# Two column units of the second block as matmuls over halves of the rows

## What is computed

```python
h = rmsnorm(x, g_mix[l])
proj = h @ w_in[l]
xc, gb, gc, q, k, v, g_sw, gate_a, gate_r = jnp.split(proj, split_points, axis=-1)
...
qf = rotary(q.reshape(b, s, RET_HEADS, RET_QK_DIM).astype(jnp.float32)) * (RET_QK_DIM ** -0.5)
kf = rotary(k.reshape(b, s, RET_HEADS, RET_QK_DIM).astype(jnp.float32))
vf = v.reshape(b, s, RET_HEADS, RET_V_DIM).astype(jnp.float32)
...
y_r = (ret.astype(dt) * jax.nn.silu(g_sw)) @ w_r_out[l]
```

## Time and profile before

| | |
|---|---|
| median of 3 runs | 900.77 us (899.85 to 902.6) |
| the profiled execution's own time | 902.56 us |
| its span | 900.4 us |
| TensorE busy | 888.9 us, 99% of the span, 5434 matmuls |
| TensorE weight loads | 761.2 us, 85% |
| VectorE, ScalarE, GpSimd busy | 608.1, 456.2, 82.9 us |
| DMA | 160.45 MB, mean 178 GB/s |

### The profile page before, as it was taken

One profiled execution on the slowest core, in us unless ns is written; L12 is line 12 of the kernel. 1 busy time (PEld: TensorE's weight loads), 2 busy tenths in 40 slices (PEclk: granted clock), 3 DMA queues, 4 the chain that ended last, 5 costly groups with the idle time before them and its releaser, 6 DMA issues.

```text
span 900.4 us, 12763 instructions
## 1 busy us (share of the span) xinstructions
PE 888.9 (99%) x5434; PEld 761.2 (85%) x5434; DVE 608.1 (68%) x734; ACT 456.2 (51%) x549; POOL 82.9 (9%) x93
## 2 busy tenths in 40 slices
PE   8999999999999999999999999999999999999997
PEld 8989788788888887888888888888888888888885
DVE  5989886776666567778858665766566566664665
ACT  6674553664445446555444365443355555444543
POOL 1001230100000000000124210110100000000000
PEclk9999999999999999999999999999999999999999
DMA  9764315146555543654564544355544456455531
GB/s 321 263 218 167 106 55 197 59 167 249 195 196 196 189 187 141 222 187 147 207 219 175 187 156 171 141 187 187 187 187 144 154 193 231 176 179 209 187 140 47
DMA packets 26089, 160.45 MB, mean 178 GB/s; under 512 B 3577, under 2 KB 4233, under 8 KB 8241
## 3 DMA queue, kind: packets, MB, share of 16 engines
q1 hardware_dynamic: 23616, 153.40, 46.8%
q0 software_dynamic: 2272, 6.24, 2.1%
q10 hardware_dynamic: 144, 0.00, 0.0%
HBM read 158.57 MB, written 2.63 MB: 179 GB/s over the span
## 4 chain that ended last, share of the span: by engine, by line
PE 83%; DVE 9%; ACT 3%; issue 2%; DMA 1%; SPq 1%; POOL 0%; POOLq 0%; DVEq 0%; ACTq 0%
PE banks L505 34%; PE banks L473 21%; PE banks L476 10%; DVE t_wl L1645 4%; PE banks L428 3%; PE banks L577 3%; PE banks L533 2%; PE banks L416 1%; PE banks L447 1%; DMA t_x<-in_x 1%; PE banks L778 1%; ACT t_wh L1155 1%; PE banks L983 1%; PE banks L1117 1%; DVE t_cv L1674 1%
## 5 line engine op out<-in xcount | busy, mean ns | idle before, releaser
L1645 DVE TENSOR_TENSOR t_wl<-t_raw,t_wh 128x2048 fp32r<-128x2048 f32 x136 | 311.7, 2313 | 109.0 <-ACT t_wh L1155 107.9
L473 PE MATMUL banks<-t_hx,t_wh 128*128 128x512 f32 x992 | 312.1, 396 | 0.0
L1155 ACT CAST t_wh<-t_raw 128x2048 fp32r<-128x2048 f32 x136 | 256.0, 1908 | 12.6 <-DMA t_raw<-in_W 7.9
L476 PEld LDWEIGHTS banks<-t_hx,t_wl 128*128 128x128 f32 x992 | 186.3, 188 | 43.7
L476 PE MATMUL banks<-t_hx,t_wl 128*128 128x256 f32 x992 | 194.9, 278 | 0.0
L473 PEld LDWEIGHTS banks<-t_hx,t_wh 128*128 128x128 f32 x992 | 153.3, 189 | 2.4
L505 PE MATMUL banks<-t_wh,t_hx 128*128 128x512 f32 x320 | 101.6, 394 | 0.0
L505 PEld LDWEIGHTS banks<-t_wh,t_hx 128*128 128x128 f32 x320 | 59.5, 188 | 12.5 <-issue 0.3
L505 PE MATMUL banks<-t_wl,t_hx 128*128 128x512 f32 x160 | 61.1, 390 | 0.0
L2293 POOL TENSOR_TENSOR t_st<-t_st,t_half 128x1 f32<-128x1 f32 (+1 forms) x18 | 10.6, 590 | 434.2 <-DVE t_st L1674 425.7
L1483 ACT COPY t_hold<-banks 128x512 f32<-128x512 f32 x28 | 16.4, 585 | 65.2 <-PE banks L476 54.6
(11 more groups left out here) (334 smaller groups left out, 1330.6 us busy)
## 6 DMA issues: line engine op xcount, KB each, us to landing
t_raw<-in_W SPq DMA_DIRECT2D x139, 1024.0 KB, 4.8
t_raw<-in_W SPq DMA_DIRECT2D x8, 256.0 KB, 6.3
t_raw<-in_W SPq DMA_DIRECT2D x4, 512.0 KB, 9.5
skew<-scr POOLq DMA_DIRECT2D x1, 1536.0 KB, 13.5
t_cout<-in_xT SPq DMA_DIRECT2D x4, 256.0 KB, 5.1
t_x<-in_x SPq DMA_DIRECT2D x2, 512.0 KB, 11.1
t_tab<-in_tab POOLq DMA_DIRECT2D x1, 640.0 KB, 7.6
out<-t_xt SPq DMA_DIRECT2D x2, 320.0 KB, 2.3
```

What stands on the lines that cost most here:

```text
L473: e.matmul(bank[b + c], M.wh[:, h, wk], M.hx[:, k, :, :].rearrange("p a s -> p (a s)"), start=k == 0, stop=False)
L476: m = e.matmul(bank[b + c][:, 0:S], M.wl[:, h, wk], M.hh[:, k, :], start=False, stop=k == 7)
L1155: e.copy(M.wh[:, h, :], M.raw[:, r, :]).then_inc(q.sem, q.tick(("hi", i)))
L1645: e.tensor_tensor(M.wl[:, h, :], M.raw[:, r, :], M.wh[:, h, :].bitcast(F32), ALU.subtract).then_inc(q.sem, q.tick(("lo", i)))
```

## The change

A function `wide_rows` takes two B units at once and multiplies them in four phases. In each phase two banks are filled for half of the rows each: the upper 64 rows of all 8 blocks go to bank f of the four, the lower 64 rows to bank f + 2 (modulo 4). So four phases give each bank both of its halves, each matmul has 64 rows in place of 128, and there are 128 of them in place of 64. At the start of phase f TensorE waits for the end of its own phase f - 2. Before phase 0 it waits for lo and for the banks of both units, and it signals both units at the end of phase 3. It replaces `wide_unit` for rot(h, 0) with rot(h, 1), and for g(h, 0) with g(h, 1): 8 pairs. A further function `a_rows`, not called anywhere, is left out of the diff below. ScalarE's, VectorE's, GpSimd's and SyncE's programs are not edited.

```diff
+            def wide_rows(tiles, arrived, by, names, places=(None, None)):
+                banks, slots = [], []
+                for tile, to in zip(tiles, places):
+                    if to is None:
+                        turn[0] += turn[0] % 2
+                    b, i = take(tile, to), next_unit()
+                    if to is None:
+                        take((tile, 1))
+                    assert PLAN[i][0] == "B" and b % 2 == 0, (i, PLAN[i], tile)
+                    q.wait_ge(DV, ("lo", i))
+                    opened(b)
+                    opened(b + 1)
+                    banks += [b, b + 1]
+                    slots.append(i)
+                for f in range(4):
+                    enter(2)
+                    for k in range(8):
+                        arrived(k)
+                        for w in range(2):
+                            for half in range(2):
+                                g = (f + 2 * half) % 4
+                                p, h, b = slice(64 * half, 64 * half + 64), slots[g // 2] % HR, banks[g]
+                                wk = slice(k * 256 + g % 2 * 128, k * 256 + g % 2 * 128 + 128)
+                                if w == 0:
+                                    e.matmul(bank[b], M.wh[p, h, wk], M.hx[p, k, :, :].rearrange("p a s -> p (a s)"),
+                                             start=f < 2 and k == 0, stop=False)
+                                else:
+                                    m = e.matmul(bank[b][:, 0:S], M.wl[p, h, wk], M.hh[p, k, :], start=False,
+                                                 stop=f >= 2 and k == 7)
+                    if f < 3:
+                        next_phase(m)
+                m.then_inc(q.sem, q.tick(*tiles, *[("unit", i) for i in slots], ("phase", phase[0])))
+                phase[0] += 1
+                for n, (b, name) in enumerate(zip(banks[::2], names)):
+                    drain(b, by, name)
+                    drain(b + 1, by, name)
...
-            def rotate(h, w):
-                wide_unit(("rot", h, w), x_mix2, DV, ("turned0", h, w))
+            def rotate(h):
+                wide_rows((("rot", h, 0), ("rot", h, 1)), x_mix2, DV, (("turned0", h, 0), ("turned0", h, 1)))
...
             for h in range(4):
-                rotate(h, 0)
-                rotate(h, 1)
+                rotate(h)
...
-            wide_unit(("g", 0, 0), x_mix2, DV, ("gsm", 0, 0))
-            wide_unit(("g", 0, 1), x_mix2, DV, ("gsm", 0, 1))
+            wide_rows((("g", 0, 0), ("g", 0, 1)), x_mix2, DV, (("gsm", 0, 0), ("gsm", 0, 1)))
...
-                for u in range(2):
-                    if h:
-                        wide_unit(("g", h, u), x_mix2, DV, ("gsm", h, u))
+                if h:
+                    wide_rows((("g", h, 0), ("g", h, 1)), x_mix2, DV, (("gsm", h, 0), ("gsm", h, 1)))
```

More of the change, by code:

```diff
@@ L388, in tensor @@
             q.begin(e)
-            free, turn, unit = [None] * 8, [0], [0]
+            free, turn, unit, phase = [None] * 8, [0], [0], [0]
             def take(tile, b=None):
@@ L483, in wide_unit, with next_phase, enter, a_rows @@
                 drain(b + 1, by, name)
+            def next_phase(last):
+                last.then_inc(q.sem, q.tick(("phase", phase[0])))
+                phase[0] += 1
+            def enter(back):
+                if phase[0] >= back:
+                    q.wait_ge(PE, ("phase", phase[0] - back))
+            def a_rows(name, act, arrived, ks, outs, first):
+                i = next_unit()
+                assert PLAN[i][0] == "A", (i, PLAN[i], name)
+                h = i % HR
+                q.wait_ge(DV, ("lo", i))
+                for k in ks:
+                    arrived(k)
+                banks = [outs[t][c] for t in range(2) for c in range(2)]
+                if first:
+                    for b in banks:
+                        opened(b)
+                for f in range(4):
+                    enter(2)
+                    for kk, k in enumerate(ks):
+                        for a, w in ((0, 0), (0, 1), (1, 0)):
+                            for half in range(2):
+                                g = (f + 2 * half) % 4
+                                p, t, c = slice(64 * half, 64 * half + 64), g // 2, g % 2
+                                m = e.matmul(bank[banks[g]][:], act[a][p, k, t * 128:t * 128 + 128],
+                                             W[w][p, h, kk * 1024 + c * 512:kk * 1024 + c * 512 + 512],
+                                             start=first and f < 2 and kk + a + w == 0, stop=False)
+                    if f < 3:
+                        next_phase(m)
+                m.then_inc(q.sem, q.tick((name, 0), (name, 1), ("unit", i), ("phase", phase[0])))
+                phase[0] += 1
```

## The result

The changed kernel takes 936.12 us (median of 4 runs, 933.45 to 938.16), the kernel before 900.58 us: a ratio of 1.0389 with a 95% interval of 1.0358 to 1.0420. The forecast was 930.0 us, with a range of 919.4 to 937.0.

The account below looks back on a forecast made before the run. TensorE was taken to bound the kernel. Waits 2.6 + 12.3 + 5.0 + 5.0, ways in and out 0.8 and clock 3.5 made 29.2 us; on the median 900.8 that gave 930.0 us, range 919.4 to 937.

Parts of the forecast that it names:

- The bound: TensorE, busy 99% of the span: whatever its stream gains or loses comes out in the time one for one.
- The pace of a couple: In the pairs, two matmuls of 64 rows side by side take as long as one of 128: no gain, no loss.
- rival 1: The waits come, and couples of 64-row matmuls run faster: 5.8 to 7.1 us less, 923.5; chance 0.32.
- rival 2: The waits come, and couples run slower, each half paying its 0.014 us: 937; chance 0.09.
- rival 3: The halves don't run side by side, so 8 pairs take 22 in place of 11 us: 1019; chance 0.05.
- One sign: In the pairs, the two matmuls of a couple start a few ns apart, couples 0.23 and 0.12 us apart.
- The joint waits: TensorE's waits around pairs, restarts included: 2.6 us at rot(0), 12.3 at three later pairs, 5.0 before and 5.0 behind g(1) to g(3).
- Rival 4: Not slower: second cast, lo and banks are ready within the 1.7 us of `scores`, no stops: 895; chance 0.04.
- In and out of 64 rows: At the pairs, 0.1 us in and 0.2 out where no wait covers it: 0.8 us behind four pairs.
- The clock: TensorE's clock slows behind the three stops of 4.0 us, 1.2 us lost for each: 3.5 us.
- The bounds of the clock: Slow-clock loss between nothing and 1.7 us for all seven long and short stops, 12 us.
- The 0.014 us per matmul over its columns: In TensorE's wide units, time beyond the columns at 2.4 GHz, about 0.014 us per matmul; its cause was left open.

Follow-up runs that it names:

- one unit at a time: The change with matmuls of 64 rows kept, but each unit on its own two banks, waiting for and freeing only its own: 909.17 us, ratio 1.0096.
- with A units: The kernel before, with the six wr units of heads 1 to 3 multiplied by halves of the rows, without joint waits: 901.53 us, ratio 1.0006.
- filled stops: The change plus 17 unread matmuls of 512 columns behind each of scores(0), scores(1) and scores(2), no wait removed: 929.38 us, ratio 1.0320.
- another order: The change with ScalarE and VectorE reordered at the rot pairs: both casts and lo before the taking-out, both takings-out before the rotations: 917.81 us, ratio 1.0194.
- neighbouring banks: The change with the two halves of the rows one bank apart in place of two, nothing else: 934.61 us, ratio 1.0379.
- with all rows: The change with every wait of the pairs kept, but multiplying with all 128 rows as before: 933.01 us, ratio 1.0361.

## Why the prediction was right, and where it was off

The mechanism was the one forecast, and the forecast was too low in two terms. Growth of each stretch of TensorE's timeline, from those transposes (357.69 and 355.74) on:

| stretch | before, us | after, us | growth | the sum had |
|---|---|---|---|---|
| to the first A unit behind rot(0) | 85.45 | 89.56 | 4.1 | 2.6 |
| to `scores(0)` | 33.04 | 33.52 | 0.5 | 0.2 |
| `scores(0)` to `scores(3)` | 38.62 | 58.53 | 19.9 | 16.4 |
| to the transposes at the end of head 0 | 26.26 | 26.36 | 0.1 | 0 |
| the rounds of heads 1 to 3 | 109.59 | 120.63 | 11.0 | 10.0 |
| to the end | 249.74 | 249.70 | 0 | 0 |
| all | 542.70 | 578.30 | 35.6 | 29.2 |

- **The bound.** TensorE's losses came out in the time one for one: behind the last pair the two kernels take the same time, and nothing gave a loss back.
- **The pace of a couple** was taken as that of a full matmul. At full clock two steps of 768 columns take 578.39 - 577.69 = 0.70 us in the changed kernel, as in the earlier trace rows:

```profile
577.69 0.43 PE L549 MATMUL banks<-t_hx,t_wh 64*128 64x512 f32 x2
...
578.39 0.44 PE L549 MATMUL banks<-t_hx,t_wh 64*128 64x512 f32 x2
```

  So rivals 1, 2 and 3 are out. One sign did not come as written: the two halves of a couple start a few ns apart only at first, and inside a pair they drift half a step apart, at an unchanged pace (one half at 444.15, the other at 444.36, the first again at 444.50).

  The Trainium skill's rule (TensorE: Matmul & The Clock Gate, "What overlaps and what doesn't"), by which halves would have hidden weight loads and won 7 us, fails here: the loads of full rows had been beside the matmuls all along, and the halves won nothing.
- **The joint waits** came as worked out: 2.8 once, 3.8 three times, 1.4 to 1.6 six times. The step to the next pair was 5.81 us for 5.7. Keeping the waits and dropping the halves left the loss; reordering ScalarE and VectorE took 18 us away. Rival 4, a stop covered by `scores`, is out by the same rows.
- **In and out of 64 rows** was put too low. rot(1) took 11.5 us with its way out, where 11.1 and 0.2 make 11.3, and the way in cost another 0.1 in front of it: 0.4 to 0.5 together for 0.3, as in the runs with one unit at a time and with A units (0.4). And the waits do not cover it, as the sum had it for the pairs of g(1), g(2) and g(3): each of these rounds grew by 3.7 us, of which 3.0 are waits. With the restarts these small terms make 2.0 us more than the sum had.
- **The clock is the term that was mis-sized.** "Part of each slow stretch falls into the stop itself, so I take 1.2 for each: 3.5." Measured: 2.4, 2.8 and 1.4 us behind the three long stops, and 1.3 behind the stop of 2.8 us, which the sum had left out: 7.9. Two of the stretches were much longer than the one in the earlier trace rows (5.5 and 6.3 us of the pair at 0.50). So the sum was 4.4 us too low in the clock and 2.0 in the ways in and out and the restarts, 29.2 + 6.4 = 35.6. That the clock caused its part behind the three long stops is shown by the run with the filled stops, 6.7 us faster.
- **The bounds of the clock** were wrong by their own numbers. There were ten stops in the list (one, three and twice three), not seven; and 12 us in place of 3.5 would have made 938.5, above the 937 at which the range ended. The measured 936.12 lies 0.9 us below that end.
- **What the clock was read from.** The prediction took the earlier trace rows to mean that thin work lowers the clock. The same stretch of the changed kernel was nearly as thin (23 matmuls from 20 to 24 us in place of 20), and the clock stayed at 1.00. That slow stretch is also most of the 1.8 us by which the profiled execution lay above the median.

What stays open: whether a given stop brings a slow stretch, and how long a one. The same stop of 2.8 us at rot(0) brought one in the profiled runs of the changed kernel, with another order, with filled stops and with neighbouring banks; it brought none with all rows, nor with the rot pairs alone. The spread of the changed kernel's runs, 4.7 us where the kernel before has 2.8, would fit that, but no run shows that.

## What to carry to other kernels

Before two pieces of work are joined into one, list what each waits for and what each frees, and then read the orders of the engines that prepare and clear: here the pair's end released a cast that stood in front of the copy for which the next pair waited, so that each long stop was 3.8 us. Matmuls over half of the rows, two at a time, were no faster here than full ones, and going over to them and back cost 0.4 to 0.5 us each time. Where TensorE must stop, count the slow clock behind the stop as well: 1.4 to 2.8 us behind each stop of 3.8 here, 1.3 or nothing behind the one of 2.8. And before two profiles are subtracted, compare them at a place in front of the change: here they were already 1.95 us apart.

## What the runs showed of the hardware that I had not expected

- **The 0.014 us per matmul over its columns was there only at the full clock.** At the low clock a step of 768 columns in the changed kernel takes its columns at 1.2 GHz and no more, 0.64 us:

```profile
485.41 0.66 PE L549 MATMUL banks<-t_hx,t_wh 64*128 64x512 f32 x2
...
486.05 0.66 PE L549 MATMUL banks<-t_hx,t_wh 64*128 64x512 f32 x2
```

  (486.05 - 485.41). Why it is there at the full clock no run here settles; that it is the same for 64 rows and for 128 is what the run with A units shows.
- **Stops of 1.4 to 1.6 us left the clock at 1.00 everywhere, a stop of 2.8 us lowered it in some runs, one of 3.8 us in every case that was not filled.** The stretch at 0.50 was longer behind some stops of 3.8 us than behind others; what decides this stays open.
